# Handover from the projection passes to retention: staging, load order, and the first head's queries

## The reference

```python
h = rmsnorm(x, mix_norm_w);  proj = h @ w_in           # q, k, v, g, a, b: 512 columns each
y_ret  = retention_group(q, k, v, g, ...)              # 4 heads of 128, both directions
y_conv = conformer_conv_group(a, b, ...)               # 31 taps, depthwise
x = x + concat(y_ret, y_conv) @ w_out
x = x + cross_attention(rmsnorm(x), rmsnorm(mem))      # 4 heads, 256 memory tokens
x = x + square(relu(rmsnorm(x) @ w_ff1)) @ w_ff2
out = rmsnorm(x, final_norm_w)
```

## Time and profile before

| | |
|---|---|
| median of 3 runs | 2923.39 us (2920.8 to 2930.39) |
| the profiled execution, time of the run | 2928.47 us |
| its span, first to last instruction | 2926.4 us |
| TensorE busy | 2803.2 us, 96% of the span |
| VectorE busy | 1371.2 us, 47% |
| GpSimd busy | 879.6 us, 30% |
| ScalarE busy | 576.0 us, 20% |
| chain that ended last, by engine | PE 81%, DVE 11%, issue 3%, DMA 2%, ACT 2%, POOL 1% |

### The profile page before, as it was taken

The page is one execution under the profiler, slowest core; times in us unless marked ns, Lnnn a source line. Parts: engine busy times, 40 slices in busy tenths (PEclk is TensorE's granted clock), DMA queues, the critical chain, the costliest instruction groups (busy, mean ns, idle before and its releaser), DMA issues.

```text
span 2926.4 us, 37167 instructions
## 1 busy us (share of the span) xinstructions
PE 2803.2 (96%) x13882; PEld 2357.4 (81%) x13882; DVE 1371.2 (47%) x1527; ACT 576.0 (20%) x1060; POOL 879.6 (30%) x439
## 2 busy tenths in 40 slices
PE   5899999998989999999999999999999999999998
PEld 4788888887767898888888888778988888888887
DVE  4593939486875333522414234433345224152343
ACT  5221212213544222100001001232221000010012
POOL 1242423344962000333333333220003333333331
PEclk8999999999999999999999999999999999999999
DMA  4133333326853222111111113132221111111111
GB/s 159 47 116 122 105 118 118 122 99 226 257 187 115 94 83 76 51 43 50 46 47 50 46 48 108 58 122 94 87 72 51 43 50 50 43 50 50 43 50 72
DMA packets 289754, 253.99 MB, mean 87 GB/s; under 512 B 8016, under 2 KB 253960, under 8 KB 283400
## 3 DMA queue, kind: packets, MB, share of 16 engines
q1 hardware_dynamic: 266320, 203.45, 22.3%
q10 hardware_dynamic: 23352, 49.39, 4.7%
HBM read 196.71 MB, written 56.10 MB: 86 GB/s over the span
## 4 chain that ended last, share of the span: by engine, by line
PE 81%; DVE 11%; issue 3%; DMA 2%; ACT 2%; POOL 1%; ACTq 0%; DVEq 0%; SPq 0%; POOLq 0%
PE ps L699 23%; PE ps L694 23%; PE ps L695 23%; DVE acc L1685 6%; PE ps L1038 2%; PE ps L1040 2%; PE ps L1039 2%; DVE st_f L1765 1%; DMA wb<-wqk_d 1%; DVE alo L1951 1%; PE ps L1000 0%; PE ps L1049 0%; PE ps L885 0%; DVE alo L1819 0%; DMA out<-rows 0%
## 5 line engine op out<-in xcount | busy, mean ns | idle before, releaser
L554 POOL TENSOR_SCALAR whi<-wraw 128x1024 fp32r<-128x1024 f32 x192 | 224.9, 1171 | 1920.1 <-PE ps L699 1189.9
L694 PE MATMUL ps<-ahi,whi 128*128 128x512 f32 x1376 | 543.0, 395 | 17.7 <-DVE alo L1951 11.5
L695 PE MATMUL ps<-alo,whi 128*128 128x512 f32 x1376 | 538.5, 391 | 0.0
L556 POOL TENSOR_TENSOR wlo<-wraw,whi 128x1024 fp32r<-128x1024 f32 x192 | 522.8, 2723 | 16.0
L694 PE MATMUL ps<-bhi,whi 128*128 128x512 f32 x1024 | 399.4, 390 | 2.3 <-DVE blo L1872 2.3
L695 PE MATMUL ps<-blo,whi 128*128 128x512 f32 x1024 | 398.4, 389 | 0.0
L1685 DVE SCALAR_TENSOR_TENSOR acc<-upad,taps,acc 128x2048 f32<-128x2048 f32 x120 | 347.8, 2898 | 15.7 <-DVE acc L1682 0.6
L699 PE MATMUL ps<-ahi,wlo 128*128 128x512 f32 x1376 | 340.1, 389 | 0.0
L694 PE MATMUL ps<-xhi,whi 128*128 128x512 f32 x768 | 305.8, 398 | 20.9 <-DVE xlo L1607 11.0
L694 PEld LDWEIGHTS ps<-ahi,whi 128*128 128x128 f32 x1376 | 259.9, 189 | 78.6 <-DVE alo L1951 14.9
L1523 ACT ACTIVATE ahi<-z 128x512 f32 x128 | 80.9, 632 | 1140.9 <-DVE z L1948 1140.9
(11 more groups left out here) (260 smaller groups left out, 3668.8 us busy)
## 6 DMA issues: line engine op xcount, KB each, us to landing
wraw<-in_w_ff SPq DMA_DIRECT2D x128, 512.0 KB, 3.7
proj_d<-st ACTq DMA_DIRECT2D x64, 256.0 KB, 2.5
wraw<-in_w_in SPq DMA_DIRECT2D x24, 512.0 KB, 4.5
xt<-in_x SPq DMA_DIRECT2D x16, 512.0 KB, 6.4
wraw<-in_w_xkv SPq DMA_DIRECT2D x16, 512.0 KB, 5.2
vwo_d<-pst ACTq DMA_DIRECT2D x16, 512.0 KB, 3.6
wqk_d<-pst ACTq DMA_DIRECT2D x16, 512.0 KB, 3.6
wraw<-in_w_out SPq DMA_DIRECT2D x16, 512.0 KB, 4.7
```

The lines of the kernel that those rows point to most:

```text
L554: pool.tensor_scalar(whi[:, slot, :, :], wraw[:, slot, :, :], 1.0, 0.0, ALU.mult, ALU.add).then_inc(w_hi, 1)
L556: pool.tensor_tensor(wlo[:, slot, :, :], wraw[:, slot, :, :], whi[:, slot, :, :], ALU.subtract).then_inc(w_ready, 1)
L694: nc.tensor.matmul(o, whi[:, slot, k, :], hi(k), start=(k == order[0]), stop=False)
L695: nc.tensor.matmul(o, whi[:, slot, k, :], lo(k), start=False, stop=False)
```

## The change

- `ORDER`: K1 stands ahead of `g1`. ScalarE's stores, VectorE's taps and the splits of K1 and T1 are put in the matching order.
- Blocks 6 and 7 of a pass are staged in `vhl` and `khl` instead of `pst`, with semaphores `pre_v` and `pre_k` of their own. ScalarE copies all four of the last blocks ahead of the store of `g3`. In the next pass it waits for `pre_k` before the position load, which lies over `khl`, and for `pre_v` before `high("V0")`.
- `v_in` and `cv_even` change places, so that the values lie over the accumulator and the first convolution chunk over `vhl` and `khl`. SP stores the accumulator right behind the straight keys' load, waits for its landing, loads the values, then the queries; the waits for the stores of blocks 4 and 5 are gone there.
- `decayed_q` works on quarters in the order in which `retained` uses them, and `retained` waits for its own quarter.
- In head 0 VectorE does eight steps of the forward scan ahead of `rotate_q`.

```diff
              "k0", "k1", "O1", "k2", "k3", "v0", "v1", "K0", "T0", "v2", "M0", "v3",
-             "g0", "g1", "K1", "T1", "g2", "M1", "g3"]
+             "g0", "K1", "g1", "T1", "g2", "M1", "g3"]
     GI, GP = {}, 0
...
             cos_t, sin_t = b2("cos_t"), b2("sin_t")
-            vb = b2("v_in")
+            cv_even = b2("cv_even", (P, CT, NC))
             kb_ = b2("k_in")
             b2("pad_room", (P, 2 * PAD + 2))
-            cv_even, ksb = b2("cv_even", (P, CT, NC)), b2("k_sw")
+            vb, ksb = b2("v_in"), b2("k_sw")
             b2("mask_room", (P, HEADS, P))
...
         pre_st = [sem("pre_st0"), sem("pre_st1")]
+        pre_v, pre_k = sem("pre_v"), sem("pre_k")
         G0 = 4
+
+        def made_in(m):
+
+            if m < 6:
+                return pst[:, m % 2, :, :]
+            return (vhl, khl)[m - 6][:, :, :, :].rearrange("p r a m -> p r (a m)")
+
         DEC_LIN = 10 + HEADS
...
             load_k(0)
-            sp.wait_ge(m_mm, 1 + 2 * HEADS)
+            conv_store(HEADS - 1)
+            sp.wait_ge(acc_st, 1 + 16 * HEADS)
             load_v(0)
-            for s in range(2):
-                sp.wait_ge(pre_st[s], 1 + 16 * (4 * HEADS - 1))
             sp.wait_ge(mm_done, G_HALF0)
             load_q(0)
-            conv_store(HEADS - 1)
-            sp.wait_ge(acc_st, 1 + 16 * HEADS)
+            sp.wait_ge(pre_v, 1 + 16 * HEADS)
+            sp.wait_ge(pre_k, 1 + 16 * HEADS)
             load_conv(0)
             for s in range(2):
-                sp.wait_ge(pre_st[s], 1 + 16 * 4 * HEADS)
+                sp.wait_ge(pre_st[s], 1 + 16 * 3 * HEADS)
             for n in range(NS):
...
                     pool.wait_ge(y_mm, 4 * h)
-                for dst, xi in ((q_f, xi_f), (q_b, xi_b)):
-                    pool.tensor_tensor(dst[:, :].rearrange("p (c q) -> p c q", q=P),
-                                       q_rot_b[:, :].rearrange("p (c q) -> p c q", q=P),
-                                       xi[:, bass.ds(h, 1), :].to_broadcast([P, CH, P]), ALU.mult).then_inc(p_qf, 1)
+                for i in DOWN:
+                    for dst, xi in ((q_f, xi_f), (q_b, xi_b)):
+                        at = slice(i * NC, (i + 1) * NC)
+                        pool.tensor_tensor(dst[:, at].rearrange("p (c q) -> p c q", q=P),
+                                           q_rot_b[:, at].rearrange("p (c q) -> p c q", q=P),
+                                           xi[:, bass.ds(h, 1), :].to_broadcast([P, 4, P]), ALU.mult).then_inc(p_qf, 1)
...
                 i = DOWN[j]
-                pe.wait_ge(p_qf, 2 * h + 2)
+                pe.wait_ge(p_qf, 8 * h + 2 * j + 2)
                 pe.wait_ge(s_ev, 4 * h + j + 1)
...
                 def made_high(m):
-                    act.wait_ge(pre_st[m % 2], 1 + 64 * c + 16 * (m // 2))
-                    act.activation(pst[:, m % 2, 0, :], ps[:, 4 + m % 4, :], ACT.Copy).then_inc(pre_hi, 1)
+                    if m < 6:
+                        act.wait_ge(pre_st[m % 2], 1 + 48 * c + 16 * (m // 2))
+                    act.activation(made_in(m)[:, 0, :], ps[:, 4 + m % 4, :], ACT.Copy).then_inc(pre_hi, 1)
...
                         dst = wqk_d[c, :, :, 2 * (m - 4):2 * (m - 4) + 2, :].rearrange("a p k m -> p a (k m)")
-                    act.dma_start(dst, pst[:, m % 2, :, :].bitcast(F32)).then_inc(pre_st[m % 2], 16)
+                    act.dma_start(dst, made_in(m).bitcast(F32)).then_inc(pre_st[m % 2] if m < 6 else pre_v if m == 6 else pre_k, 16)
...
                 wait_alone(act, m_mm, 1 + 2 * c)
+                wait_alone(act, pre_k, 1 + 16 * c)
                 act.dma_start(pos_i[:, :], positions[0:1, bass.ds(c * NC, NC)].to_broadcast([P, NC])).then_inc(tab_in, 16)
...
                 wait_alone(act, o_mm, 1 + 2 * c)
+                wait_alone(act, pre_v, 1 + 16 * c)
                 high("V0", vhl[:, 0, 0, :])
...
                 store("v", 8, 2, 3)
-                store("g", 12, 0, 1)
+                store("g", 12, 0)
                 high("K1", khl[:, 1, 0, :])
+                store("g", 12, 1)
                 query_high(1)
...
                 made(4)
+                made(6)
                 store("g", 12, 3)
-                made(6)
             leave_phase(act)
...
                         act.wait_ge(s_mm, 4 * HEADS)
+                        act.wait_ge(p_qf, 8 * HEADS)
                         if k >= HEADS:
...
                 query_low(0)
-                taps_of(21, TAPS)
+                taps_of(21, 28)
                 low("K1", 3, khl[:, 1])
+                taps_of(28, 30)
                 query_low(1)
+                taps_of(30, TAPS)
                 for m in range(4, 8):
...
+            def straight_q0():
+                dve.wait_ge(l_q, 16)
+                dve.wait_ge(l_cos, 16)
+                dve.tensor_tensor(qb_[:, :], qb_[:, :], cos_t[:, :], ALU.mult).then_inc(r_q, 1)
+
             def rotate_q(h):
                 if h == 0:
-                    dve.wait_ge(l_q, 16)
-                    dve.wait_ge(l_cos, 16)
-                    dve.tensor_tensor(qb_[:, :], qb_[:, :], cos_t[:, :], ALU.mult).then_inc(r_q, 1)
                     dve.wait_ge(r_q, 1)
...
                     dve.wait_ge(p_qc, h)
-                    dve.wait_ge(p_qf, 2 * h)
+                    dve.wait_ge(p_qf, 8 * h)
                 dve.wait_ge(p_qs, h + 1)
...
-            def forward_scan(h):
+            def forward_scan(h, first=0, last=CH - 1):
...
                     dve.wait_ge(y_mm, 4 * h)
-                for c in range(CH - 1):
+                for c in range(first, last):
                     if c % 4 == 0:
...
             dve.memset(st_b[:, CH - 1, :], 0.0).then_inc(zero_st, 1)
-            rotate_q(0)
+            straight_q0()
             dve.wait_ge(dec_act, DEC_EXP)
...
                 last = h + 1 == HEADS
-                forward_scan(h)
+                if h == 0:
+                    forward_scan(0, 0, 8)
+                    rotate_q(0)
+                    forward_scan(0, 8)
+                else:
+                    forward_scan(h)
                 for j in range(4):
```

More of the change, by code:

```diff
@@ L1167, in _ @@
         def _(act):
-            start_at_one(act, tab_st, acc_st, o_mm, m_mm, *pre_st, *st_st)
+            start_at_one(act, tab_st, acc_st, o_mm, m_mm, pre_v, pre_k, *pre_st, *st_st)
             at = 0
@@ L1674, in made_low @@
                     dve.wait_ge(pre_hi, 8 * c + m + 1)
-                    dve.tensor_tensor(pst[:, m % 2, 1, :], ps[:, 4 + m % 4, :], pst[:, m % 2, 0, :], ALU.subtract).then_inc(pre_lo, 1)
+                    dve.tensor_tensor(made_in(m)[:, 1, :], ps[:, 4 + m % 4, :], made_in(m)[:, 0, :], ALU.subtract).then_inc(pre_lo, 1)
                 def tap(t):
```

## The result

The changed kernel takes 2943.47 us in the median of five runs (2940.11 to 2944.88); the kernel before, with its further runs on the same chip, 2925.5. The ratio is 1.0058, interval 1.0047 to 1.0069: 17 us slower, where 9.4 were forecast and the range ended at 2940. The profiled execution has a span of 2942.9 us against 2926.4.

The account below looks back on a forecast made before the run. TensorE was taken to bound the passes, DMA and GpSimd's chain the handover and head 0's end. Terms 5.1 + 2.5 + 0.9 + 0.9 = 9.4 us on the median 2923.39 gave 2932.8 us; range about 2922 to 2940.

Parts of the forecast that it names:

- K1: Projection passes: moved K1 product waits 1.7 us a pass for GpSimd's low split; +5.1 us for three passes.
- The handover: After the last pass: store lands at 705, values 7.0 us later, rotated queries at 727.2 against 724.73; +2.5 us.
- Quarters in head 0: Head 0: GpSimd's eight shorter decays delay head 1's swapped keys and `rotate_k(1)`; +0.87 us.
- Quarters in heads 1 and 2: Heads 1 and 2: GpSimd idles for the rotated queries, so its longer decays cost 0.
- rival 1: End of head 0: TensorE waits for `rotate_k(1)`, its clock falls; +1.9, transposes +0.5; sum 11.8, 2935.2 us; chance 0.22.
- Last head: Head 3: longer decays count through weight splits and gate into the reload of that output; +0.87 us.
- Dead tiles' new waits: Next pass and last phase: ScalarE's added waits on `pre_k`, `pre_v` and the decays cost 0.
- Rival 2: Handover: accumulator's store lands early, at 701.2, rotated queries at 723.3; sum 5.5, 2928.9 us; decides from 704.4; chance 0.20.
- Rival 3: Passes: K1's low split is ready before 681.4, so TensorE does not stand; sum 2.6 to 4.3, 2927 us; chance 0.08.

Follow-up runs that it names:

- (16): The kernel before with K1 moved one group forward alone; 2929.78 us, 1.0015 against the kernel before.
- (1): The changed kernel with K1, its store, taps and copies put back behind `g1`; 2937.3 us, 1.0047 against the kernel before.
- (13): The changed kernel without the accumulator's store at the handover (its convolution output is another one); 2936.97 us, 1.0039 against the kernel before.
- (9): The changed kernel with GpSimd's product on the next head's swapped queries waiting for that head's rotated keys; 2939.09 us, 1.0046 against the kernel before.
- (10): The kernel before with quarters, and GpSimd's product on the next head's swapped queries waiting for that head's rotated keys; 2926.52 us, 1.0002.
- (6): The kernel before with the decays by quarters alone; 2930.08 us, 1.0020 against the kernel before.
- (11): The kernel before with quarters, GpSimd's swapped-query product waiting for the rotated keys, and TensorE's outputs held for all eight decays; 2926.32 us, 1.0003.
- (15): The kernel before with quarters, TensorE's outputs held for all eight decays, no wait for the rotated keys; 2931.88 us, 1.0026.
- (3): The changed kernel with the old handover (last split products staged, tiles laid and transfers ordered as before); 2937.56 us, 1.0040 against the kernel before.
- (2): The changed kernel with the decayed queries as two whole-tile products again; 2934.76 us, 1.0040 against the kernel before.
- (5): The kernel before with the new staging, tile places and order of the handover's transfers alone; 2930.69 us, 1.0030.

## Why the prediction was wrong

**K1: right.** The stand was put at 1.7 us a pass and released by GpSimd's low split; it is 1.5, with that releaser, and passes are 1.5 to 1.6 longer. For four passes (16) gives 4.4 us, and (1) 3.2 by the ratios and 6.2 by the medians.

**The handover: the order of the waits right, three durations too small; 6.9 us, the largest part of the miss.** The step that failed reads "Then `load_v` ... lands 7.0 us later, the nearest and least of its landings", with the store's landing and the queries' span ahead and behind it. The store took 10.0 us where 8.3 were walked (696.7 to 705), the values 9.7 for 7.0, and from the values' issue to the swapped queries lay 20.7 us (707.58 to 728.27) for 14.1. From the store's issue to these queries that is 30.7 for 22.5. The queries' own landing near 18.7 us is above the upper bound stated, 18.3. The bounds of the store and of the values held the measured times; the values were priced at the least of theirs, the store below the middle of its own, and the queries by the kernel before plus the bytes of the values, while the forecast itself put more on a full queue. Nothing in the walk stands for the convolution chunk and the next head's keys, which are now loaded while the queries land. (13) shows that the lateness goes with the store; how much of the last leg is the chunk's load stays open.

**Quarters in head 0: right,** 0.84 for 0.87. **Quarters in heads 1 and 2: the step whose mechanism failed, 3.6 us.** It reads "In heads 1 and 2 GpSimd idles for the rotated queries (13.9 us in four heads): 0". For the 0.87 itself this holds: with the places kept, heads 1 and 2 take 38.9 us with quarters too, in (1), (9) and (10). What the 0 left out is who goes first where VectorE's rotation and GpSimd's next product meet. The forecast had that meeting in its text ("it waited out one whole GpSimd instruction") and took for granted that the wait is for one. It can be for two. (10) against (6), 1.8 per mille, and (11) against (15), 2.3, put 5 to 7 us on it in the kernel before, with the clock that a lost place can cost; (9) against the change, 1.2, fits, with overlapping intervals. By the Trainium skill, SBUF — State Buffer, section "Who interferes with whom", an engine that has the shared port pair keeps it for a whole instruction, which these rows bear out, and the one that issues first gets it; by that VectorE, begun at 793.70, should go before a product that starts at 795.86. VectorE goes first where GpSimd's swapped product takes 6.59 us, and does not where it takes 4.50, so the rule does not settle the order here.

**The clock: rival 1 came true.** The forecast's own sum has nothing for it: "frees TensorE by some us, but TensorE then waits for `rotate_k(1)`". Rival 1 took up that wait, and it cost 1.74 of the 2.4 us given, after a stand of 1.97 us where 4.7 were walked (748 to 752.7). The experiments add where the stand comes from: not from late queries, since (3) has it with early ones and (2) lacks it with late ones, but from TensorE's early end, by the split scan and the quarters together. What was called their gain turns into the stand. The clock also fell without it, in (5) and (15), and whether a stand near 2 us costs the clock is not settled by these runs (below).

**Last head:** 0.53 for 0.87. **Dead tiles' new waits:** 0, right by (5). **Rival 2** (early loads) is out: a store landing near 707.6, not before 704.4. **Rival 3** is out: the moved product stood in all four passes.

Open: why short decays raise the odds of a lost place from 1 in 15 to 13 in 21. The start of the rotation within GpSimd's straight product does not tell: in head 0 it is 0.2 us in kept and lost ones alike (754.22 against 754.05, kept; in (6) 742.64 against 742.45, lost).

## What to carry to other kernels

A store that must land before a load may go out puts its whole landing, on a queue as full as it will then be, ahead of everything behind that load; when the change itself adds to the queue, carry the slower landings of each leg through the sum, and list every transfer that will then be under way beside it. Cutting an operation of one engine into pieces that free another gained nothing here, where a third sets the end, and it cost twice: in the order of two engines on a shared path, and in the clock of the engine freed. Idle time covers a longer operation, but not a change in who goes first where the two engines meet.

## What the runs showed that was not expected

- A VectorE sum of two 128x2048 tiles takes 2.29 us alone, 3 to 6.5 beside GpSimd's products of 4.5, and 7.6 to 11 when GpSimd's next product goes first, with the same instructions.
- A stand of TensorE near 2 us is followed by either level of the clock (1.2 or 2.4 GHz). In (11) the second half of the key transposes starts after 2.17 us idle and the variance products behind it take 3.79 us, at 1.00 granted; in (5) after 1.92 us, and they take 5.29, at 0.72. The second halves, in (11) and in (5):

```profile
748.84 1.14 PE L860 MATMUL ps<-ident,k_rot 128*128 128x128 f32 x8 [2.17 <-ACT k_tok L1354]
```

```profile
752.00 1.14 PE L863 MATMUL ps<-ident,k_rot 128*128 128x128 f32 x8 [1.92 <-ACT k_tok L1360]
```

- A stretch that no kernel here touches differs by up to 3.8 us between profiled executions: GpSimd's third weight split starts between 61.2 and 65.0. The runs of the kernel before lie up to 12.5 us apart (2920.49 to 2933.0).
